# Step sizes as one fp32 product on four column groups, and two heads' mixing products side by side

## What is computed

```
h    = rmsnorm(x, ln1_g)                       # per token 1/rms, times a gain per channel
dt   = softplus(h @ w_dt + dt_bias)            # 4 heads, one step size per head and token
a    = -exp(a_log) * dt                        # cumulated in chunks of 128 tokens
S    = (C B^T) * exp(segsum(a))                # per head and chunk, 128 x 128
y    = S @ (x*dt)  +  (C * exp(cumsum a)) @ state_of_the_chunk_before
out  = rmsnorm((y + d*x) * silu(z), norm_g)
```

## Time and profile before

| | |
|---|---|
| median of 3 runs | 1403.04 us |
| the profiled execution | 1402.84 us |
| its span (first to last instruction) | 1401.1 us |
| TensorE matmuls busy | 1354.3 us, 97% of the span |
| VectorE / ScalarE / GpSimd busy | 66% / 36% / 49% |
| mean granted TensorE clock | 0.99 |

### The profile page before, as it was taken

The page is one execution under the profiler, slowest core; times in us unless marked ns, Lnnn a source line. Parts: engine busy times, 40 slices in busy tenths (PEclk is TensorE's granted clock), DMA queues, the critical chain, the costliest instruction groups (busy, mean ns, idle before and its releaser), DMA issues.

```text
span 1401.1 us, 15858 instructions
## 1 busy us (share of the span) xinstructions
PE 1354.3 (97%) x6130; PEld 1058.0 (76%) x6130; DVE 924.5 (66%) x1239; ACT 503.7 (36%) x754; POOL 686.2 (49%) x370
## 2 busy tenths in 40 slices
PE   7999998899999999999999999989999999999999
PEld 4877566677788888888878765657778888888887
DVE  8879987666788506776237798966577772177730
ACT  5432334655332212323334324445562322123221
POOL 2836897114444444444456378941244444444442
PEclk9999999999999999999999999999999999999999
DMA  6321111113333322323233211111132333233332
GB/s 218 96 61 61 60 48 51 34 42 84 104 93 104 119 78 91 104 91 114 81 108 95 69 46 60 60 46 30 40 113 91 103 104 103 81 95 102 96 111 94
DMA packets 34091, 118.43 MB, mean 85 GB/s; under 512 B 3936, under 2 KB 4064, under 8 KB 34016
## 3 DMA queue, kind: packets, MB, share of 16 engines
q1 hardware_dynamic: 34016, 117.42, 26.6%
HBM read 114.26 MB, written 2.10 MB: 83 GB/s over the span
## 4 chain that ended last, share of the span: by engine, by line
PE 88%; DVE 9%; ACT 1%; issue 1%; POOL 1%; DMA 0%; SPq 0%; DVEq 0%; POOLq 0%
PE bank L423 26%; PE bank L436 25%; PE bank L428 24%; PE bank L490 1%; PE bank L425 1%; PE bank L636 1%; PE bank L499 1%; PE bank L465 1%; PE bank L595 1%; PE bank L597 1%; PE bank L617 1%; PE bank L627 1%; PE bank L449 1%; DVE bank L1055 1%; DVE ml L1061 1%
## 5 line engine op out<-in xcount | busy, mean ns | idle before, releaser
L318 POOL TENSOR_TENSOR wl<-raw,wh 128x1024 fp32r<-128x1024 f32 (+3 forms) x208 | 501.2, 2410 | 633.1 <-ACT wh L771 390.7
L423 PE MATMUL bank<-xl,wh 128*128 128x512 f32 x1152 | 303.3, 402 | 1.7 <-DVE xl L1022 1.1
L771 ACT ACTIVATE wh<-raw 128x1024 fp32r<-128x1024 f32 (+3 forms) x208 | 218.5, 1051 | 236.3 <-PE bank L428 204.1
L436 PE MATMUL bank<-xh,wl 128*128 128x512 f32 x1152 | 285.9, 390 | 0.0
L428 PE MATMUL bank<-xh,wh 128*128 128x512 f32 x1120 | 277.7, 390 | 0.0
L423 PEld LDWEIGHTS bank<-xl,wh 128*128 128x128 f32 x1152 | 215.7, 190 | 72.7 <-issue 25.3
L436 PEld LDWEIGHTS bank<-xh,wl 128*128 128x128 f32 x1152 | 216.0, 188 | 45.1 <-issue 0.3
L428 PEld LDWEIGHTS bank<-xh,wh 128*128 128x128 f32 x1120 | 211.2, 189 | 44.3
L1065 DVE TENSOR_TENSOR x<-x,bank 128x512 f32<-128x512 f32 x64 | 44.0, 688 | 225.1 <-PE bank L436 225.1
L423 PE MATMUL bank<-ml,wh 128*128 128x512 f32 x512 | 139.9, 401 | 0.0
L436 PE MATMUL bank<-mh,wl 128*128 128x512 f32 x512 | 127.5, 389 | 0.0
(11 more groups left out here) (275 smaller groups left out, 1497.2 us busy)
## 6 DMA issues: line engine op xcount, KB each, us to landing
raw<-in_w_gu SPq DMA_DIRECT2D x88, 512.0 KB, 3.5
raw<-in_w_in SPq DMA_DIRECT2D x52, 512.0 KB, 3.5
raw<-in_w_dn SPq DMA_DIRECT2D x32, 704.0 KB, 4.1
raw<-in_w_oe SPq DMA_DIRECT2D x16, 384.0 KB, 3.0
raw<-in_w_ol SPq DMA_DIRECT2D x16, 256.0 KB, 2.6
x<-in_x SPq DMA_DIRECT2D x8, 256.0 KB, 6.8
raw<-in_w_first SPq DMA_DIRECT2D x4, 512.0 KB, 4.8
out_x<-x SPq DMA_DIRECT2D x8, 256.0 KB, 5.1
```

Source lines behind the costliest of these rows:

```text
L318: tt(wl[:, p, 0:cols], raw[:, p, 0:cols], wh[:, p, 0:cols].bitcast(F32), ALU.subtract).then_inc(wl_full, 1)
L423: mm(bank[b][:, :], wh[:, p, k * P:(k + 1) * P], lo[:, k, :], start=(k == 0), stop=False)
L436: w = mm(bank[b][:, :], wl[:, p, k * P:(k + 1) * P], hi[:, k, :], start=False, stop=(k == K - 1))
L771: fn(wh[:, p, 0:cols], raw[:, p, 0:cols], ACT.Copy).then_inc(wh_full, 1)
```

## The change

The step-size product takes the unsplit fp32 `x` in place of `xh` and `xl`, with the gain multiplied into the weights. The weights are padded with zeros from 4 to 32 columns; the eight slices of the contraction go round the four 32-column groups of the array, so that each group ends with the sum of two slices in its 32 partitions of bank 5. The scaling by 1/rms runs on 128 partitions. A product with a 0/1 matrix `pick` (1 where the row modulo 32 is the column) adds the four groups and turns them at once. The padded weights lie in the memory of `hst`, which is not in use then.

`m2_apply(i)` now does heads 2i and 2i+1 in alternation. Pair 0 stands behind unit 12 and waits for both heads' mixes; pair 1 stands inside unit 15. `m2_pair(l, 1)` moves from VectorE's step 14 to 15, between `sc_gate(1)` and `emit_low`, and `m2_square(1)` from ScalarE's step 14 to 15, after `emit`.

```diff
-        wdth = sb("wdth", [P, KD, M2H], F32R)
-        wdtl = sb("wdtl", [P, KD, M2H], F32R)
+        wdt = sb("wdt", [P, KD, SH], at=offsets["hst"])
@@ TensorE
-                for n, (a, b) in enumerate(((wdth, xl), (wdth, xh), (wdtl, xh))):
-                    for k in range(KD):
-                        w = mm(bank[5][0:M2H, :], a[:, k, :], b[:, k, :], start=(n == k == 0),
-                               stop=(n == 2 and k == KD - 1))
+                for k in range(KD):
+                    r = SH * (k % 4)
+                    w = mm(bank[5][r:r + SH, :], wdt[:, k, :], x[:, k, :], start=(k < 4), stop=(k >= 4))
...
-                    w = nc.tensor.transpose(bank[5][:, t * M2H:(t + 1) * M2H], G[0:M2H, 5, t * P:(t + 1) * P],
-                                            ident[0:M2H, 0:M2H])
+                    w = mm(bank[5][:, t * M2H:(t + 1) * M2H], G[:, 5, t * P:(t + 1) * P], pick, start=True, stop=True)
...
-            def m2_apply(h):
-                pe.wait_ge(mix_ready, nth(mix_ready))
-                if h == 0:
+            def m2_apply(i):
+                pe.wait_ge(mix_ready, nth(mix_ready, 2))
+                if i == 0:
                     pe.wait_ge(*free_at[7])
                     pe.wait_ge(*free_at[5])
-                if h % 2 == 0:
-                    claim(5, yz_ready)
-                r = slice(M2P * (h % 2), M2P * (h % 2) + M2P)
+                claim(5, yz_ready)
+                heads = [(2 * i + e, slice(M2P * e, M2P * e + M2P), *m2buf[e]) for e in range(2)]
                 for t in range(NQ):
                     c = slice(t * P, (t + 1) * P)
-                    decayed, decayed_c = m2buf[h % 2]
-                    w = mm(bank[5][r, c], xbt[:, t, h // 2, r], decayed[:, c], start=True, stop=(t == 0))
+                    for h, r, decayed, _ in heads:
+                        w = mm(bank[5][r, c], xbt[:, t, i, r], decayed[:, c], start=True, stop=(t == 0))
                     if t > 0:
-                        w = mm(bank[5][r, c], hst[:, t - 1, h, :], decayed_c[:, c], start=False, stop=True)
-                w.then_inc(mix_read, 1)
+                        for h, r, _, decayed_c in heads:
+                            w = mm(bank[5][r, c], hst[:, t - 1, h, :], decayed_c[:, c], start=False, stop=True)
+                w.then_inc(mix_read, 2)
...
-                    if s == 11:
-                        m2_apply(0)
+                    if s == 14:
+                        m2_apply(1)
...
                     if s == 12:
-                        m2_apply(1)
+                        m2_apply(0)
                         s5_out(0)
                         m2_decays(2)
                         m2_scores(1)
                     if s == 13:
-                        m2_apply(2)
                         m2_decays(3)
-                    if s == 14:
-                        m2_apply(3)
@@ ScalarE
                     if s == 14:
                         emit(MIXB, G[:, 4, :])
-                        m2_square(1)
                     if s == 15:
                         emit(MIXB + 1, G[:, 5, :])
+                        m2_square(1)
@@ VectorE
-                copy(flat(wdth[:]), w)
+                after(nc.vector.memset(wdt[:, :, :], 0.0))
+                gain = par_of(l, "g1", 0, KD).unsqueeze(2).broadcast_to([P, KD, M2H])
...
-                tt(flat(wdtl[:]), w, flat(wdth[:]).bitcast(F32), SUB).then_inc(wdt_ready, 1)
+                tt(wdt[:, :, 0:M2H], w, gain, MUL).then_inc(wdt_ready, 1)
...
-                tt(G[0:M2H, 5, :], bank[5][0:M2H, :], rbc[0:M2H, :], MUL).then_inc(dve_free[5], 1)
+                tt(G[:, 5, :], bank[5][:, :], rbc[:, :], MUL).then_inc(dve_free[5], 1)
...
+                    if s == 15:
+                        m2_pair(l, 1)
                     if s == 14:
-                        m2_pair(l, 1)
                         s5_scan(l, 1)
```

More of the change, by code:

```diff
@@ L45 @@
 CONSTS, _o = {}, 0
-for _name, _n in [("ident", P), ("ones", P), ("tri", P), ("perm", P), ("block", P), ("cap", P)]:
+for _name, _n in [("ident", P), ("ones", P), ("tri", P), ("perm", P), ("block", P), ("cap", P), ("pick", 4)]:
     CONSTS[_name] = slice(_o, _o + _n)
@@ L166, in build @@
             cst[:, CONSTS[k]] for k in ("ident", "ones", "tri", "perm", "block", "cap")]
+        pick = cst[:, CONSTS["pick"]]
         cosT, sinT = rotary[:, 0, :], rotary[:, 1, :]
@@ L1076, in parameters @@
             def parameters(l):
-                w = par_of(l, "wdt", 0, KD * M2H)
-                copy(flat(wdth[:]), w)
+                w = par_of(l, "wdt", 0, KD * M2H).rearrange("p (k h) -> p k h", k=KD)
+                after(nc.vector.memset(wdt[:, :, :], 0.0))
+                gain = par_of(l, "g1", 0, KD).unsqueeze(2).broadcast_to([P, KD, M2H])
                 ts(par_of(l, "subg"), par_of(l, "subg"), par_of(l, "oneml"), None, MUL)
                 after(ts(par_of(l, "qkg"), par_of(l, "qkg"), QK ** -0.5, None, MUL))
-                tt(flat(wdtl[:]), w, flat(wdth[:]).bitcast(F32), SUB).then_inc(wdt_ready, 1)
+                tt(wdt[:, :, 0:M2H], w, gain, MUL).then_inc(wdt_ready, 1)
             def turn_matrices(l):
@@ L1588, in constants @@
     c[:, CONSTS["block"]] = r[:, None] // QK == r[None, :] // QK
+    c[:, CONSTS["pick"]] = r[:, None] % SH == np.arange(M2H)[None, :]
     c[:, CONSTS["cap"]] = np.where(r[None, :] >= r[:, None], 0.0, NEG)
```

## The result

The changed kernel takes 1390.05 us (median of 5 runs, 1389.23 to 1395.1) against 1403.04 us of the kernel before run beside it (5 runs): ratio 0.9913, 95% interval 0.9898 to 0.9928. The forecast was 1389.8 us. The total came out within 0.3 us of it, the terms did not: that they cancel is luck, and the experiments are about the terms.

The account below looks back on a forecast made before the run. TensorE was taken as the bound (busy 97%, 88% of the chain), except where VectorE has the chain. 2.85 + 3.15 + 2 x 3.6 = 13.2 us off 1402.84 gave 1389.6, median 1389.8 us; range 1386 to 1395.5.

Parts of the forecast that it names:

- Step-size product: Step-size matmuls on TensorE: four column groups side by side, 2.1 us instead of 5.56, a gain of 3.5 us a layer.
- turning: Turning behind the step sizes: four two-pass products take 0.9 us; net loss 0.35 us a layer, after 0.2 us back.
- VectorE's part between the layers: VectorE's `parameters` for layer 1: some 0.3 us more, hidden by its 0.56 us wait for a down-projection unit.
- Rivals 1: Step-size product: only two column groups work at a time, 1.8 us less gain per layer; 1393.4 us, chance 0.13.
- rival 3: Step sizes and mixing pairs: no column groups work side by side, gain about zero; 1403 us, chance 0.03.
- "Is the gain kept?", layer 0: Layer 0's step-size stretch: VectorE starts unit 2's work 3.3 us earlier; 2.85 us kept, GpSimd hits zero +-2 us.
- Rival 2: VectorE gives less: mixing brings 2 us a layer, layer 0 loses 2 us more to GpSimd hits; 1395 us, chance 0.12.
- Mixing: Mixing products: paired heads take one head's time and VectorE's waits from 107 to 144 us shrink; 3.6 us gained a layer.
- rival 4: The clock fall at 163 to 170 us goes, about 3 us a layer; 1384 us, chance 0.07.
- Rival 5: The clock falls earlier, near `m2_norm`, and lasts until 170 us: +22 us a layer, minus 7; 1433 us, chance 0.02.
- My signs: Observations named beforehand as showing the forecast right or wrong; a granted clock below 1 before 150 us meant wrong.
- Other signs: Signs of being right: layer 0's unit 13 starting at about 107 us; the clock fall as before, about 6.5 us earlier.

Follow-up runs that it names:

- before_fill18: Kernel before the change, plus fp32 products nobody reads in TensorE's two waits behind unit 18; 1397.8 us, ratio 0.9971.
- fill: Changed kernel plus fp32 products nobody reads, one between the two products of `m2_norm` and two behind it; 1391.91 us, ratio 0.9922.
- heads_in_turn: Changed kernel with the two heads of a pair written one after the other instead of alternating; 1394.62 us, ratio 0.994.

## Why the prediction was right in the sum and wrong in its terms

- **Step-size product, turning, VectorE's part between the layers: right.** 1.85 us against 2.1, turning 0.79 against 0.9, layer 1 3.19 against 3.15. The longer `parameters(1)` is hidden as forecast: VectorE's wait shrank from 0.56 to 0.24 us. Rivals 1 and 3 are refuted: four groups take 1.85 us, where two take 3.56 and one 6.98. The order rule from which rival 3 was drawn was read too strictly: the same section of the Trainium skill ("TensorE: Matmul & The Clock Gate", Part 3) reports a speed-up of 2.38 for three column tiles. Here four groups gave 6.98 / 1.85 = 3.8.
- **"Is the gain kept?", layer 0: wrong.** I took the risk of GpSimd hits as +-2 us around zero and forecast 2.85 us. I looked at one instruction that was already slow (2.21 us) and not at what lay next to it when all moved 3 us ahead: eight short instructions in front of a pair of 2.4 us subtractions. VectorE lost 5.1 us there and got 2.0 us back further on (the product L1276 took 0.17 us, where it took 2.19 before, L1280). The clock fall, which is in no term, took the first run of the next unit from 2.09 to 3.66 us. In all the layer came out 4.2 us below the forecast. By these rows the price of such a meeting is up to the rest of one GpSimd instruction for each VectorE instruction that falls into one. Rival 2 had such hits in layer 0, at 2 us, but the weaker mixing part that it went with did not come.
- **Mixing: the mechanism right, the size not.** The waits of the earlier trace rows went as listed. Their part can be read at the product with z in step 16 (L1502 before, L1499 after): it started 60.90 us behind `m2_states` (144.32 - 83.42) and now starts 57.66 us behind it (141.70 - 84.04). So VectorE's waits gave 3.2 us, against 3.6. The rest came from the fall behind unit 18, which I had put down to rival 4 at 0.07, "about 3 us a layer". Its price was right (2.9 us, by `before_fill18`): less the 0.67 us that the new fall costs, it gives the 2.2 us left in layer 0, and in layer 1, where VectorE keeps the chain beside the fall at unit 17, 2.9 us stand against 2.7 left.

  The argument against it, that TensorE gains as much as VectorE, was wrong. Counted from `m2_states`, before the change TensorE was ready for the product with `qk` at 75.44 us and `qk` at 77.76. After it `qk` is ready at 72.42 us in layer 0 and at 74.63 in layer 1, and TensorE, held up by its new waits and the slow unit 17, only at 76.29 and 74.75. So the wait is gone in both layers.

  In layer 0 VectorE was faster still, because two of its steps now miss GpSimd: the pair of L1056 takes 1.29 us instead of 2.40 and L1366 0.74 instead of 1.77, since GpSimd, which worked without a gap from 153.87 to 161.33 us before, now stands idle until 154.14. It is not what removed the wait, for in layer 1 both are as slow as before (2.40 and 1.77 us). And `fill` shows the other side: with unit 17 at full clock TensorE is ready at 73.23 us and waits again. The timeline of VectorE before, then after:

```profile
155.03 2.40 DVE L1061 TENSOR_TENSOR ml<-xbc,mh 128x512 fp32r<-128x512 f32 x2 [1.54 <-ACT mh L808]
157.34 1.77 DVE L1370 SCALAR_TENSOR_TENSOR qk<-G,par_all,rotary 128x512 f32<-128x512 f32 x1
```
```profile
152.44 1.29 DVE L1056 TENSOR_TENSOR ml<-xbc,mh 128x512 fp32r<-128x512 f32 x2 [0.45 <-ACT mh L803]
153.65 0.74 DVE L1366 SCALAR_TENSOR_TENSOR qk<-G,par_all,rotary 128x512 f32<-128x512 f32 x1
...
155.77 0.69 DVE L1371 TENSOR_TENSOR qk<-bank,G 128x512 f32<-128x512 f32 x1
```

- **Rival 5 was half right.** The clock does fall earlier, at the place it names. But it recovers by 149 us instead of lasting to 170, and with VectorE close behind it costs 0.67 us, not 22. My signs had it as "wrong if the granted clock is below 1 before 150 us": it is, and the total held all the same. Other signs failed too: unit 13 of layer 0 starts at 110.48 us and not at about 107, by what that layer lost ahead of it, and the clock fall did not stay as before.
- **The fall as such.** With the waits filled it is gone from that place, in both kernels, so without TensorE standing still it does not come. But the waits alone do not decide it. Two waits of 0.81 and 1.78 us with one product between them are followed by a fall (between the waits of the earlier trace rows, too, stands one product in two passes, not two products); the wait of 0.79 us ahead of the pair, by itself, is not. Waits of 1.4 and 0.80 us brought one in layer 1 of `fill` and none in layer 0; a wait of 1.69 us brought one in layer 1 of `heads_in_turn` and none in layer 0. What else decides is open.

Open: the stretch between the layers varied from 469.8 to 471.4 us over the kernels, though of all the edits only `parameters(1)` lies in it, which is hidden. And why the same waits bring a clock fall in one layer and not in the other is not shown.

## What to carry to other kernels

A gain of some microseconds on one engine moves everything behind it against the other engines. List what the shift brings together: VectorE's casts, scalings and two-operand products between SBUF tiles, however short, in a stretch where VectorE has the chain and GpSimd runs, and put such work where VectorE waits anyway. Price a clock fall by how close the next engine is behind TensorE at that place: one cost 0.7 us where VectorE took the chain over as soon as it was gone, and 2.9 us where TensorE then ran on without a wait. And a small fp32 product with few output columns, its contraction spread over four column groups, took a quarter of its time on one group (1.85 against 6.98 us) and a third of the split form's 5.56 us.

## What the hardware showed that I had not expected

- Four fp32 products in four column groups run with no loss that shows: 16 passes of 512 columns in 1.85, 3.56 and 6.98 us on four, two and one group.
- A VectorE instruction of 128x2 elements took 2.29 us beside GpSimd and 0.16 us without it; a 128x128 cast 2.42 against 0.22 us.
- Idle work can pay: some 2.2 us of products that nobody reads, put into TensorE's waits, made the kernel before 4 us faster.
